# A hybrid decoder trunk on one core: the second mixer's projection in the 512-column form, with ScalarE copying a half bank, transposes one piece later, and norms that take the root first

## The reference

```
h += mixer(rmsnorm(h)); h += swiglu(rmsnorm(h)); h += sigmoid(rmsnorm(h) W_g) * (p[i] W_p)
```

```
z, xbc, dt = split(u @ w_in)                      # 4096, 6144, 64 columns
xbc = silu(causal_dwconv(xbc, conv_w, conv_b))    # 4 taps
xs (64 heads x 64), B, C (8 groups x 128) = split(xbc)
y = ssd_scan(xs, softplus(dt + bias), A, B, C) + d_skip * xs
y = y * silu(z); y = y * rsqrt(mean over its group of 512 (y*y) + eps) * norm_g
out = y @ w_out
```

## Time and profile before

| what | us |
|---|---|
| median of 3 runs (lowest, highest) | 2685.89 (2684.47, 2686.33) |
| the profiled execution's own time | 2685.37 |
| its span, first to last instruction | 2683.7 |
| PE busy | 2658.5 (99%) |
| DVE busy | 2001.5 (75%) |
| ACT busy | 1376.0 (51%) |
| POOL busy | 283.2 (11%) |

### The profile page before, as it was taken

One profiled execution on the slowest core, in us unless ns is written; L12 is line 12 of the kernel. 1 busy time (PEld: TensorE's weight loads), 2 busy tenths in 40 slices (PEclk: granted clock), 3 DMA queues, 4 the chain that ended last, 5 costly groups with the idle time before them and its releaser, 6 DMA issues.

```text
span 2683.7 us, 47807 instructions
## 1 busy us (share of the span) xinstructions
PE 2658.5 (99%) x16831; PEld 2389.3 (89%) x16831; DVE 2001.5 (75%) x2805; ACT 1376.0 (51%) x1869; POOL 283.2 (11%) x314
## 2 busy tenths in 40 slices
PE   9999999999999999999999999999999999999998
PEld 8999888888888888899998999988888888888887
DVE  7788776665666678889996799978666566667776
ACT  6776444444444445556664566644444444444454
POOL 1001300000000111100001000032000000001211
PEclk9999999999999999999999999999999999999999
DMA  6545565556655566655555655555555665555564
GB/s 215 183 168 193 184 199 188 188 175 189 203 190 190 190 194 196 185 178 193 190 193 181 204 182 192 193 182 189 191 188 174 188 205 190 190 188 176 187 202 138
DMA packets 154237, 504.62 MB, mean 188 GB/s; under 512 B 17104, under 2 KB 21520, under 8 KB 152976
## 3 DMA queue, kind: packets, MB, share of 16 engines
q1 hardware_dynamic: 154048, 503.14, 57.9%
q10 hardware_dynamic: 80, 0.07, 0.0%
HBM read 500.97 MB, written 2.16 MB: 187 GB/s over the span
## 4 chain that ended last, share of the span: by engine, by line
PE 89%; DVE 5%; ACT 3%; issue 2%; DMA 1%; SPq 0%; DVEq 0%; ACTq 0%
PE bank L419 51%; PE bank L421 26%; PE bank L401 4%; PE bank L403 4%; PE bank L402 4%; DVE wlo L923 2%; ACT whi L629 1%; DVE arena L1131 1%; DMA wraw<-in_A 0%; ACT L707 0%; PE bank L592 0%; DVE R L1024 0%; ACT arena L707 0%; ACT arena L716 0%; PE bank L583 0%
## 5 line engine op out<-in xcount | busy, mean ns | idle before, releaser
L419 PE MATMUL bank<-R,whi 128*128 128x512 f32 x5984 | 2083.4, 394 | 0.1
L421 PE MATMUL bank<-R,wlo 128*128 128x256 f32 x5984 | 1662.6, 278 | 0.0
L923 DVE TENSOR_TENSOR wlo<-wraw,whi 128x1024 fp32r<-128x1024 f32 (+2 forms) x1008 | 1164.0, 1161 | 547.4 <-ACT whi L629 545.9
L629 ACT ACTIVATE whi<-wraw 128x1024 fp32r<-128x1024 f32 (+2 forms) x1008 | 984.3, 983 | 912.8 <-PE bank L421 810.4
L419 PEld LDWEIGHTS bank<-R,whi 128*128 128x128 f32 x5984 | 1122.0, 188 | 259.9 <-DVE wlo L923 0.4
L421 PEld LDWEIGHTS bank<-R,wlo 128*128 128x128 f32 x5984 | 1124.8, 188 | 0.1
L401 PE MATMUL bank<-R,whi 128*128 128x256 f32 x1376 | 393.2, 286 | 5.5 <-DVE wlo L923 5.2
L403 PE MATMUL bank<-R,wlo 128*128 128x256 f32 x1376 | 389.5, 283 | 0.0
L402 PE MATMUL bank<-R,whi 128*128 128x256 f32 x1376 | 389.4, 283 | 0.0
L401 PEld LDWEIGHTS bank<-R,whi 128*128 128x128 f32 x1376 | 262.5, 191 | 10.2 <-DVE wlo L923 5.6
L402 PEld LDWEIGHTS bank<-R,whi 128*128 128x128 f32 x1376 | 262.7, 191 | 0.2
(11 more groups left out here) (177 smaller groups left out, 1271.7 us busy)
## 6 DMA issues: line engine op xcount, KB each, us to landing
wraw<-in_F SPq DMA_DIRECT2D x352, 512.0 KB, 3.3
wraw<-in_B SPq DMA_DIRECT2D x224, 512.0 KB, 3.3
wraw<-in_A SPq DMA_DIRECT2D x96, 512.0 KB, 3.8
wraw<-in_F SPq DMA_DIRECT2D x128, 384.0 KB, 3.1
wraw<-in_F SPq DMA_DIRECT2D x128, 320.0 KB, 3.2
wraw<-in_PL SPq DMA_DIRECT2D x64, 512.0 KB, 4.0
arena<-cs_rows SPq DMA_DIRECT2D x8, 1024.0 KB, 5.7
arena<-in_gates SPq DMA_DIRECT2D x8, 512.0 KB, 3.7
```

Source lines behind the costliest of these rows:

```text
L419: nc.tensor.matmul(dst.rearrange("p (s t) -> p s t", s=2), whi[:, q % RING, cols], src[:, :, k, :], start=first, stop=False)
L421: mm = nc.tensor.matmul(dst[:, 0:SEQ], wlo[:, q % RING, cols], src[:, 0, k, :], start=False, stop=last)
L629: nc.scalar.activation(whi[:, slot, 0:w * BLOCK], wraw[:, slot, 0:w * BLOCK], ACT.Copy).then_inc(w_hi, 1)
L923: V.tensor_tensor(wlo[:, slot, 0:w * BLOCK], wraw[:, slot, 0:w * BLOCK], whi[:, slot, 0:w * BLOCK].bitcast(F32), ALU.subtract).then_inc(w_ ...
```

## The change

Every piece of B1 takes the wide form. In each odd step ACT first waits for PE to finish the piece, copies the bank's second half to `low_half` (two buffers), and counts half_done. DVE waits for that and adds the first half (PSUM) and the copy (SBUF), for all ten tiles, and then multiplies by rinv or rinvh. The taps of the convolution are interleaved with other work instead of each waiting for the one before: in an even step the second tap, the silu of the tile before, the third tap; in the next odd step the add, the last tap, the multiply. The last tap of tile 5 is thus in step 13, and its silu in step 14, behind lo(17). PE's product of B and C and the transposes move behind piece 15, DVE's reading of them to step 16, the two score products to steps 17 and 18.

Norms take the root first: ACT's Sqrt reads the statistics in PSUM, with the scale and eps in the instruction; DVE then takes the reciprocal. In a group of the mixer the Sqrt is in step 5 and the reciprocal in step 7, ahead of the norm multiplies (in B2, steps 4 and 5). At the end of the kernel a Sqrt of one element is put ahead of the last gain, rinv is copied to PSUM for DVE, DVE multiplies 12 tiles, POOL 4. POOL sets `eps` at the start, and PE and ACT wait for that as well.

```diff
-WIDE = ("A2", "F1", "F2", "B2")
-LAST = ((0, 4), (4, 4), (8, 4), (12, 2), (14, 2))
+WIDE = ("A2", "B1", "F1", "F2", "B2")
+LAST = ((0, 3), (3, 3), (6, 3), (9, 2), (11, 1))
+LAST_POOL = ((12, 2), (14, 2))
...
# PE
-                    if ph["name"] not in WIDE and not (ph["name"] == "B1" and q >= 12 or gate):
+                    if ph["name"] not in WIDE and not gate:
...
-                            if q == 14:
+                            if q == 15:
                                 pe.wait_ge(silu_done, group * 6 + 6)
...
# ACT
             def norm(k):
-                act.wait_ge(var_done, k + 1)
-                nc.scalar.activation(rinv[:], rinvh[:], ACT.Sqrt).then_inc(rinv_done, 1)
+                act.wait_ge(stats_done, k + 1)
+                nc.scalar.activation(rinvh[:], bank[6][:, 0:SEQ], ACT.Sqrt, bias=eps[:, 0:1], scale=1.0 / D
+                                     ).then_inc(root_done, 1)
...
+                            if q % 2 == 1:
+                                act.wait_ge(w_used, p + 1)
+                                act.wait_ge(bank_free, it * 10 + ph["group0"] + 4 + q // 2 - 1)
+                                nc.scalar.activation(low_half[:, q // 2 % 2, :], bank[BANKS4[q // 2 % 4]][:, SEQ:2 * SEQ],
+                                                     ACT.Copy).then_inc(half_done, 1)
...
-                            if q == 6 and not first:
-                                group_rinv(group - 1)
+                            if q == 5 and not first:
+                                group_root(group - 1)
...
+            nc.scalar.activation(spare[:], ones[:, 0:1], ACT.Sqrt)
             gain(KT - 1)
             norm(6)
# DVE
             def norm(k):
-                dve.wait_ge(stats_done, k + 1)
-                own.link(V.tensor_scalar(rinvh[:], bank[6][:, 0:SEQ], 1.0 / D, EPS, ALU.mult, ALU.add))
-                V.reciprocal(rinvh[:], rinvh[:]).then_inc(var_done, 1)
-                dve.wait_ge(rinv_done, k + 1)
...
+                dve.wait_ge(root_done, k + 1)
+                own.link(V.reciprocal(rinv[:], rinvh[:]))
                 own.link(V.tensor_scalar(rinvh[:], rinv[:], 0.5, None, ALU.mult))
...
+                        if name == "B1" and q == 14:
+                            conv_silu(it + ph["half"] * 4, 5)
...
                             if q % 2 == 0 and 2 <= q <= 12:
                                 nt = q // 2 - 1
                                 dve.wait_ge(tap_done, group * 6 + nt + 1)
-                                later_taps(cpad[:, nt % 2], ca[:, nt, :],
...
+                                second = tap(group, nt, 2)
+                                if nt:
+                                    conv_silu(group, nt - 1)
+                                own.need(second)
+                                third = tap(group, nt, 1)
                             if q % 2 == 1:
...
+                                tile = q // 2
+                                dst = cpad[:, tile % 2, 3:3 + SEQ] if tile < 6 else zt[:, tile - 6, :]
+                                dve.wait_ge(half_done, group * 10 + tile + 1)
...
+                                folded = own.mark(V.tensor_tensor(dst, bank[BANKS4[tile % 4]][:, 0:SEQ], low_half[:, tile % 2, :],
+                                                                  ALU.add))
+                                if 1 <= tile <= 6:
+                                    own.need(third)
+                                    last_tap(group, tile - 1)
+                                own.need(folded)
+                                V.tensor_tensor(dst, dst, rinv[:] if tile < 6 else rinvh[:], ALU.mult).then_inc(bank_free, 1)
...
-                            if q == 14:
+                            if q == 16:
                                 dve.wait_ge(turned, group + 1)
...
-                            if q in (15, 17):
-                                h0 = 0 if q == 15 else 4
+                            if q in (17, 18):
+                                h0 = 0 if q == 17 else 4
...
                 def group_norm(group):
-                    dve.wait_ge(grinv_done, group + 1)
+                    dve.wait_ge(groot_done, group + 1)
+                    own.link(V.reciprocal(grms[:], grms[:]))
...
-            norm(6)
+            dve.wait_ge(root_done, 7)
+            V.reciprocal(rinv[:], rinvh[:]).then_inc(rinv_last, 1)
+            dve.wait_ge(rinv_last, 1)
+            own.link(V.tensor_copy(bank[7][:, 0:SEQ], rinv[:]))
...
# POOL
+            pool.wait_ge(rinv_last, 1)
+            pool.wait_ge(gained, KT)
+            for m, n in LAST_POOL:
+                G.tensor_tensor(h[:, m:m + n, :], gained_h[:, m:m + n, :],
+                                rinv[:].rearrange("p (a t) -> p a t", a=1).broadcast_to([P, n, SEQ]), ALU.mult
+                                ).then_inc(out_ready_pool, 1)
```

More of the change, by code:

```diff
@@ L391, in _, with store @@
                         body(it, False)
-            for c, (m, n) in enumerate(LAST):
+            def store(m, n):
+                sp.dma_start(out[:, m:m + n, :], h[:, m:m + n, :]).then_inc(out_done, 16)
+            for c, part in enumerate(LAST):
+                if c in (2, 4):
+                    sp.wait_ge(out_ready_pool, c // 2)
+                    store(*LAST_POOL[c // 2 - 1])
                 sp.wait_ge(out_ready, c + 1)
-                sp.dma_start(out[:, m:m + n, :], h[:, m:m + n, :]).then_inc(out_done, 16)
-            sp.wait_ge(out_done, 16 * len(LAST))
+                store(*part)
+            sp.wait_ge(out_done, 16 * (len(LAST) + len(LAST_POOL)))
         @block.tensor
@@ L896, in y_square, with group_root @@
                     nc.scalar.activation(ysq, zt, ACT.Square).then_inc(ysq_done, 1)
-                def group_rinv(group):
-                    act.wait_ge(gvar_done, group + 1)
-                    nc.scalar.activation(grms[:], grms[:], ACT.Sqrt).then_inc(grinv_done, 1)
+                def group_root(group):
+                    act.wait_ge(gstat_mm, group + 1)
+                    nc.scalar.activation(grms[:], bank[7][:, 0:SEQ], ACT.Sqrt, bias=eps[:, 0:1], scale=1.0 / 512
+                                         ).then_inc(groot_done, 1)
                 def group_hi(group, local):
@@ L1195, in body @@
                                 group_y(ph["half"] * 4 + 3)
-                            if q == 4:
-                                group_var(ph["half"] * 4 + 3)
                             if q == 5:
@@ L1301, in body @@
                                 group_y(group - 1)
-                            if q == 5 and not first:
-                                group_var(group - 1)
                             if q == 7 and not first:
@@ L1359, in body, with weight_of, tap, last_tap @@
                                                 .broadcast_to([P, 4, SEQ]), ALU.mult).then_inc(sc_done, 1)
+                def weight_of(group, nt, k):
+                    return flat(bpar[:, at(group), nt * 5 + k:nt * 5 + k + 1])
+                def tap(group, nt, k):
+                    return own.mark(V.scalar_tensor_tensor(out=ca[:, nt, :], in0=cpad[:, nt % 2, k:k + SEQ],
+                                                           scalar=weight_of(group, nt, k), in1=ca[:, nt, :],
+                                                           op0=ALU.mult, op1=ALU.add))
+                def last_tap(group, nt):
+                    V.scalar_tensor_tensor(out=ca[:, nt, :], in0=cpad[:, nt % 2, 0:SEQ], scalar=weight_of(group, nt, 0),
+                                           in1=ca[:, nt, :], op0=ALU.mult, op1=ALU.add).then_inc(conv_done, 1)
+                def conv_silu(group, nt):
+                    dve.wait_ge(conv_t, group * 6 + nt + 1)
+                    V.scalar_tensor_tensor(out=ca[:, nt, :], in0=cth[:, nt % 2, :], scalar=1.0,
+                                           in1=ca[:, nt, :], op0=ALU.add, op1=ALU.mult).then_inc(silu_done, 1)
                 def z_silu(group, j):
@@ L1383, in group_y @@
                         V.tensor_tensor(zt[:, j, :], ca[:, 2 + j, :], zt[:, j, :], ALU.mult).then_inc(yz_done, 1)
-                def group_var(group):
-                    dve.wait_ge(gstat_mm, group + 1)
-                    own.link(V.tensor_scalar(grms[:], bank[7][:, 0:SEQ], 1.0 / 512, EPS, ALU.mult, ALU.add))
-                    V.reciprocal(grms[:], grms[:]).then_inc(gvar_done, 1)
                 def group_norm(group):
-                    dve.wait_ge(grinv_done, group + 1)
+                    dve.wait_ge(groot_done, group + 1)
+                    own.link(V.reciprocal(grms[:], grms[:]))
                     for j in range(4):
@@ L1394, in group_norm @@
                                                in1=grms[:], op0=ALU.mult, op1=ALU.mult).then_inc(yn_done, 1)
-                steps(dve, ph, body, own, {"A1": 14, "B1": 26, "F1": 6, "PL": 0, "F2": 4}.get(name, 8))
+                steps(dve, ph, body, own, {"A1": 14, "B1": 32, "F1": 6, "PL": 0, "F2": 4}.get(name, 8))
```

48 lines of the change are left out of this document (17 added, 31 removed).

## The result

The changed kernel takes 2728.59 us (median of 5 runs, 2725.36 to 2729.99) against 2685.89 us: ratio 1.0153, 95% interval 1.0141 to 1.0164. It is slower, as forecast, but by 42.7 us where 20 were forecast, and outside the range. The profiled execution has a span of 2727.2 us, 43.5 more than before, and a mean granted clock of 0.992 instead of 0.998.

What follows compares the result with a forecast made beforehand. PE, busy 99% of the span, was taken as the bound, with DVE and ACT close behind. Norm groups +20.3, half-two opener +0.9, first group +2 and ends -2.3 gave +20.9 on 2685.37: 2706 us, range 2687 to 2714.

Steps and rivals of the forecast that it cites:

- Part 1: Pieces 0 to 11 of each B1 group: the wide form's faster block pace saves 9.6 us in all, bounds 5.4 and 11.5.
- Parts 2 and 3: Behind piece 15: the copy delays Relu, Exp and tile 5's silu; PE waits 1.6 us in the group without norm.
- T(5): The end of piece 5 of a group, from which the forecast counts times; other numbers in brackets mean other pieces.
- Part 4: Reciprocal in step 7 makes DVE late: PE waits 3.9 us behind piece 15; weights for pieces 11 and 12 cost nothing.
- Part 5: Second half of the score product in step 18: PE waits 0.67 us in each of 8 groups, 5.4 us.
- Part 6: First group, where PE already waits 2.6 us for a silu: +2 us net, bounds 0 and +5.
- Part 7: Ends of the kernel: tail -1.2 us from fewer DVE multiplies, first stage -1.1 us from the norm.
- The sum: Six norm groups +3.4 us each, group opening half two +0.9, first group +2, ends -2.3: together +20.9 us.
- bare chains: Rival: PE waits only 0.85 and 0.67 us a group, without lateness from Relus or reciprocal; 2685.5 us, chance 8%.
- works off the lateness: Rival: Relus are late but the reciprocal's lateness is recovered, 1.6 us of waiting in each group; 2694 us, chance 20%.
- the faster one: Rival: the stretch fits and PE never waits, so only the pace's and the ends' savings stay; 2673.5 us, chance 10%.
- worse: Rival: DVE so late that lo(11) and lo(12) stop PE as well, 1 to 2 us a group more; 2714 us, 7%.

Runs made afterwards that it cites:

- filler run: The changed kernel with 8 useless matmuls for PE behind piece 15, ahead of its wait for the silu: 2717.33 us, ratio 1.0117.
- four moves: The changed kernel with reciprocal back in step 5, Relu and Exp before the copy, tile 5's silu and step 18's score product before lo: 2678.42 us, ratio 0.9969.
- Relus ahead: The changed kernel with ACT's Relu and Exp of steps 11, 13, 15 and 17 ahead of the half-bank copy: 2708.09 us, ratio 1.0084.
- silu ahead: The changed kernel with DVE's silu of tile 5 ahead of lo(17) in step 14: 2718.71 us, ratio 1.0115.
- norms alone: The kernel before with only the root-first norms and the tail, B1's forms and order untouched: 2685.72 us, ratio 0.9993.

## Why the prediction was right in its way and wrong in its size

- Part 1, the pace: right where nothing stops PE. Blocks of the wide form go at 353 ns behind the mixing matmuls and at 347 behind the statistics. Not foreseen: behind PE's stop ahead of piece 11 in three of the six groups, and behind the transposes in two of the eight, it is 353 again.
- Parts 2 and 3, the chain to the silu: the mechanism is right. Forecast 3.9 us of waiting in a group with a norm, 1.6 in the one without; measured 3.3 to 3.9 and 1.25, counted from PE's recorded end, which lies 0.16 us behind the start of what would follow. That 3.9 came out so well is partly luck: in the group of the timelines the silu ends 32.6 us behind T(5) = 1311.59, not 31.6, and T(15) is 29.0 behind it, not 27.7. The ends are 1.0 and 1.3 us late, and their difference hides it.
- Part 4: right that the reciprocal adds lateness, wrong that the weights of pieces 11 and 12 are just in time and cost nothing. Piece 11 stops PE 0.6 to 1.1 us in the six groups with a norm, 4.5 us together. lo(11) ends at T(5)+14.7 and not +13.6. The working put POOL's slowing of DVE at 1.1 us and on the taps alone; the rows at 1323.07 to 1324.51 lose 1.2 us ahead of lo(11)'s end (the last tap 0.63 for 0.47, the multiply 0.95 for 0.42, lo(11) 1.76 for 1.22). Before, the multiply read PSUM and kept its 0.42 beside POOL; the change's fold made it one that reads SBUF twice.
- Part 5: forecast 0.67 us, measured 0.3 to 0.5.
- Part 6, the first group: forecast +2 us. Its first mixing matmul starts 3.1 us later while the phase begins 1.7 us earlier, so +4.8. Its wait behind piece 15 is 4.76 us, the longest.
- Part 7: first stage -1.7 instead of -1.1. The tail gives nothing instead of -1.2: the multiplies are 1.1 us shorter, and seven stores at a median of 0.58 us of issue each take it. DVE and POOL did not hinder each other: 12 tiles in 3.61 us are 0.30 us a tile, as the 16 in 4.70 before, beside POOL's 2.49 us.
- The sum: six groups were forecast at +3.4 and came at +6.1 to +7.6, 39.4 us instead of 20.3. The group that opens the second half was forecast at +0.9, and it is +0.9 (151.76 against 150.87 us).

The step that failed is the sum for the six groups with a norm. On the profiled executions +20.9 us were forecast and +43.5 measured, so 22.6 are missing, 19.1 of them in these groups (39.4 for 20.3). First, PE's wait was priced at its own length and what follows it at nothing: behind a wait of over 3 us the transposes and the first wide blocks ran at a lower granted clock. The filler run gives its size, some 11.9 us in these groups, with the wait's end unmoved. Second, Part 4 had lo(11) just in time and free: its stops give 4.5 us. These are 16 of the 19.1 us; the rest, 3 us, is in small terms that no run separates, the paces among them. The other 3.5 us lie ahead of the first mixing matmul (+3.1 us for +0.9) and in the tail (+0.1 for -1.2).

Of the rivals, the "bare chains" and "works off the lateness" cases fell with the measured 3.3 to 3.9 us, the faster one with them. The "worse" case, with a chance of 7%, was the nearest: lo(11) does stop PE (lo(12) does not), and its 2714 us was still too low, since it too left the clock out.

## What to carry to other kernels

A saving of PE time in a PE-bound stretch is only as good as the slack of the in-order queues behind it; write out, for each point where PE waits, the last instructions of the other engines in program order, and count the ones ahead of it that nobody wants yet. Here four moves past such work, one of which takes back the reciprocal's new place, turned +1.5% into -0.3%. When one wait is removed, look at the next point that hangs on the same backlog before adding up the gain. And price an idle stretch of TensorE above its length: what follows it may run at half the clock.

## What the runs showed of the hardware

- The granted clock and PE's idle time. The measure is the time from L578 (L568) to the next wide block, 1.46 to 1.56 us at the full clock. Behind 3.3 to 4.8 us of idle it was 2.4 to 3.0 us in seven cases and 1.75 in one. Behind 2.8 to 3.1 us it was 2.35 to 3.0 in nine and 1.56 in three; behind 2.0 to 2.6 us 1.7 to 3.0 in seven and 1.56 in five; behind 1.8 us and less it was never above 1.56. So the loss differs between like waits, and no run here settles on what it hangs.
- Two paces of the same matmuls, 347 and 353 ns a block, at the full granted clock. The pace changes nearly always where PE's stream is interrupted; in three runs (filler, Relus ahead, silu ahead) it once changed 3 us behind a stop, between two blocks like all others. In the run with the norms alone it cost 0.25 us a group with nothing else changed on PE. Why isn't known.
- DVE beside POOL's splits: instructions with two inputs in SBUF took 0.95 us instead of 0.42 (multiply of 256 columns) and 1.76 instead of 1.22 (1024 columns), while the add at 1322.74, with one input in PSUM, kept its 0.42.
- ACT's copy of 128x256 from PSUM takes 0.36 to 0.39 us, less than the 0.40 to 0.42 of a tanh from SBUF, and the next instruction starts 0.26 to 0.28 us behind its start.
